# The two norms around mixer 2 made in halves of 256 tokens, with some weight low parts moved to GpSimd

## The reference, cut to what matters

```python
# end of block 1
x = x + 0.5 * swiglu(rms_norm(x, ffn2_norm), ffn2_w_gate, ffn2_w_up, ffn2_w_down)
# block 2
sh1, sc1, g1, sh2, sc2, g2 = jnp.split(mod, 6, axis=-1)
h = _rms(x, norm1_w) * (1 + sc1) + sh1                  # norm "p1"
u, q, k, v = jnp.split(h @ w_in, ...)                   # "q2" is computed first
... # S5 and sliding-window attention give "mixed"
x = x + g1 * (mixed @ w_out)                            # "w_out2"
h2 = _rms(x, norm2_w) * (1 + sc2) + sh2                 # norm "p2"
x = x + g2 * _conv_ffn(h2, w_up, conv_w, conv_b, w_down)  # "ffn3"
```

## Time and profile before

| | |
|---|---|
| median of 3 runs | 1794.73 us (1794.62 to 1794.98) |
| the profiled execution | 1793.39 us, its span 1791.9 us |
| PE busy | 1763.9 us, 98% |
| DVE busy | 1069.7 us, 60% |
| ACT busy | 729.3 us, 41% |
| POOL busy | 186.1 us, 10% |
| granted clock of PE | 0.999 over the span |

### The profile page before, as it was taken

How to read it: one execution, slowest core, us unless ns; L and a number is a source line. 1 busy time by engine, 2 the same in 40 slices (tenths; PEclk the granted TensorE clock), 3 DMA queues, 4 the chain that set the end, 5 groups by cost and what they waited for, 6 DMA issues and landing times. The chain is left out here.

```text
span 1791.9 us, 23429 instructions
## 1 busy us (share of the span) xinstructions
PE 1763.9 (98%) x8822; PEld 1437.1 (80%) x8822; DVE 1069.7 (60%) x1507; ACT 729.3 (41%) x1001; POOL 186.1 (10%) x239
## 2 busy tenths in 40 slices
PE   9999999999999999999999999999999999999998
PEld 6888888888887777788877888887986788888887
DVE  7666546655655676656888743436595655566433
ACT  4222222333435877423333222225465355555322
POOL 4222001210000000005211110210000300000000
PEclk9999999999999999999999999999999999999999
DMA  7777423343222121224554552325122222222232
GB/s 246 238 221 221 134 74 96 98 138 99 90 95 94 48 66 53 71 94 150 173 188 125 158 158 66 107 93 187 68 79 68 93 95 94 94 94 82 94 95 81
DMA packets 171694, 206.81 MB, mean 115 GB/s; under 512 B 18404, under 2 KB 150114, under 8 KB 171106
## 3 DMA queue, kind: packets, MB, share of 16 engines
q1 hardware_dynamic: 144994, 161.97, 27.9%
q0 software_dynamic: 12640, 38.55, 6.7%
q10 hardware_dynamic: 13984, 5.27, 1.1%
HBM read 190.29 MB, written 17.56 MB: 116 GB/s over the span
## 5 line engine op out<-in xcount | busy, mean ns | idle before, releaser
L692 ACT CAST w_hi<-w_raw 128x2048 fp32r<-128x2048 f32 x158 | 301.8, 1911 | 722.4 <-PE bank L2004 360.9
L1188 DVE TENSOR_TENSOR w_lo<-w_raw,w_hi 128x2048 fp32r<-128x2048 f32 x158 | 367.3, 2325 | 358.4 <-ACT w_hi L692 357.7
L2004 PE MATMUL bank<-h_hi,w_hi 128*128 128x512 f32 x1056 | 412.3, 390 | 3.5 <-DVE w_lo L1188 2.2
L2004 PE MATMUL bank<-h_hi,w_lo 128*128 128x512 f32 x1056 | 411.1, 389 | 0.0
L2004 PE MATMUL bank<-h_lo,w_hi 128*128 128x512 f32 x1056 | 325.4, 389 | 1.6 <-DVE h_lo L1231 1.6
L2004 PEld LDWEIGHTS bank<-h_hi,w_hi 128*128 128x128 f32 x1056 | 198.2, 188 | 49.5 <-issue 3.4
L2004 PEld LDWEIGHTS bank<-h_lo,w_hi 128*128 128x128 f32 x1056 | 198.2, 188 | 43.3 <-DVE h_lo L1231 2.0
L2004 PEld LDWEIGHTS bank<-h_hi,w_lo 128*128 128x128 f32 x1056 | 198.3, 188 | 41.0
L1961 PE MATMUL bank<-hid_hi,w_hi 128*128 128x512 f32 x528 | 205.6, 389 | 0.0
L1961 PE MATMUL bank<-hid_hi,w_lo 128*128 128x512 f32 x528 | 205.4, 389 | 0.0
L1961 PE MATMUL bank<-hid_lo,w_hi 128*128 128x512 f32 x528 | 205.4, 389 | 0.0
(11 more groups left out here) (442 smaller groups left out, 2464.8 us busy)
## 6 DMA issues: line engine op xcount, KB each, us to landing
w_raw<-in_w_in SPq DMA_DIRECT2D x29, 1024.0 KB, 5.0
mod_raw<-in_w_mod POOLq DMA_DIRECT2D x96, 256.0 KB, 4.1
w_raw<-in_ffn_w_gate SPq DMA_DIRECT2D x22, 1024.0 KB, 5.2
w_raw<-in_ffn_w_up SPq DMA_DIRECT2D x22, 1024.0 KB, 5.2
w_raw<-in_w_up SPq DMA_DIRECT2D x22, 1024.0 KB, 4.9
w_raw<-in_ffn_w_down SPq DMA_DIRECT2D x16, 768.0 KB, 4.6
w_raw<-in_ffn_w_down SPq DMA_DIRECT2D x16, 640.0 KB, 4.0
w_raw<-in_w_out SPq DMA_DIRECT2D x8, 1024.0 KB, 5.0
```

The lines of the kernel that those rows point to most:

```text
L692: act.copy(w_hi[i % 2][:], w_raw[i % 2][:]).then_inc(S("w_hi_done"), 1)
L1188: dve.tensor_tensor(w_lo[s][:], w_raw[s][:], w_hi[s][:].bitcast(F32), ALU.subtract).then_inc(S("w_split"), 1)
L2004: mm = pe.matmul(bank[:], w[:, k, at], h[:, k, :], start=k == first and part == 0 and i == 0, stop=k == last and part == 1)
```

## The change

Both norms are cut into two halves of 256 tokens.

- **First half early.** The last product group before each norm is made half by half. In `ffn2`, tiles 6 and 7 are closed one panel earlier, DVE adds that part to `x` (512 wide), and the last panel goes, half by half, to other banks and is added by `half_x2`. In `w_out2`, tile 7 is made in two halves. PE issues the three sums of half 0 between the two halves (`half_sums`).
- **Items.** The norm then makes 16 items (k, half) of 128 x 256, in the order of `ITEMS`. DVE issues the adds for half 1 among the first items, and refines half 1's root after item 3.
- **Products.** `q2` is made item by item in both its panels, 512 columns to a product as before. Step 0 of `ffn3` is made by `first_step`: all its products have 256 columns, and parts of the up panel stand between gate items 4 to 7.
- **Low parts on POOL.** The low parts of three weight panels (both of `q2`, and the up panel of `ffn3`'s step 0) are made by POOL (`low_part`) instead of DVE. POOL's load of `bias` comes after two of them.
- **The rest.** ACT loads the table of the reciprocal root ahead of norm p1 with a small activation; the 18 idle products are gone; the cast of the up panel of `ffn3`'s step 0 is made in two pieces with an item between.

```diff
...
+        HALF = [slice(c * T // 2, (c + 1) * T // 2) for c in range(2)]
+        IN_HALVES = {"ffn2": 2, "mix2": 1}
+        ITEMS = {"p1": [(k, c) for ks in (range(4), range(4, KD)) for c in range(2) for k in ks],
+                 "p2": [(k, c) for c in range(2) for k in range(KD)]}
+        HALF_SUMS = 3
+        HALF_SQ = {"p1": 4, "p2": 3}
...
+        def last_bank(k, c):
+            return B[((4, 6), (5, 4))[k % 2][c]]
+        def tile7_bank(c):
+            return B[(0, 4)[c]]
+        def half_sum(name, c):
+            return B[{"p1": (7, 5), "p2": (7, 6)}[name][c]][:, HALF[c]]
+        def slot(s):
+            return tmp[:, 2 + (s // 2 + 2) % 4, HALF[s % 2]]
...
+            def low_part(n):
+                pool.wait_ge(S("w_hi_done"), n + 1)
+                pool.wait_ge(S("w_split"), n)
+                pool.tensor_tensor(w_lo[n % 2][:], w_raw[n % 2][:], w_hi[n % 2][:].bitcast(F32), ALU.subtract).then_inc(S("w_split"), 1)
             norm("p1", "ffn2")
+            low_part(BASE["mix2"])
+            low_part(BASE["mix2"] + 1)
             wait_x(pool, "ffn2", KD - 1)
             pool.wait_ge(S("band_stored"), 16 * BESIDE_STEPS)
             pool.dma_start(bias[:], bass.AP(band_dram, P - 1, [[BAND - 1, P], [P * BAND, NQ], [1, 2 * P]])).then_inc(S("bias_landed"), 16)
             norm("p2", "mix2")
+            low_part(BASE["ffn3"] + 1)
...
+            def half_square(before, k, halves):
+                wait_x(act, before, k, halves[-1])
+                at = slice(HALF[halves[0]].start, HALF[halves[-1]].stop)
+                act.activation(tmp[:, 2 + k % 2, at], x[:, k, at], ACT.Square).then_inc(S("norm_sq"), 1)
+            def half_root(name, c):
+                act.wait_ge(S("norm_summed"), NORM_SUM[name] + HALF_SUMS * (c + 1))
+                act.activation(rstd[:, HALF[c]], half_sum(name, c), ACT.Abs_reciprocal_sqrt, scale=1.0 / D, bias=eps_col).then_inc(S("norm_root"), 1)
+            def half_cast(name, shift, items):
+                for s in items:
+                    k, c = ITEMS[name][s]
+                    act.wait_ge(S("norm_h"), NORM_H[name] + s + 1)
+                    act.activation(h_hi[:, k, HALF[c]], slot(s), ACT.Identity, bias=shift(k)).then_inc(S("norm_hi"), 1)
...
-            norm("p1", x, lambda eng, k: wait_x(eng, "ffn2", k), panel=BASE["mix2"] + 1, shift=lambda k: mod[:, k:k + 1])
+            done(act.activation(stat[:, 95:96], eps_col, ACT.Abs_reciprocal_sqrt))
+            shift1 = lambda k: mod[:, k:k + 1]
+            half_square("ffn2", 6, (0, ))
+            half_square("ffn2", 7, (0, ))
+            half_root("p1", 0)
+            half_cast("p1", shift1, (0, 1))
+            split(BASE["mix2"] + 1)
+            half_square("ffn2", 6, (1, ))
+            half_square("ffn2", 7, (1, ))
+            half_cast("p1", shift1, (2, 3))
+            half_root("p1", 1)
+            half_cast("p1", shift1, range(4, 2 * KD))
...
-            norm("p2", x, lambda eng, k: wait_x(eng, "mix2", k), panel=BASE["ffn3"] + 1, shift=lambda k: mod[:, 24 + k:25 + k])
+            shift2 = lambda k: mod[:, 24 + k:25 + k]
+            half_square("mix2", 6, (0, 1))
+            half_square("mix2", 7, (0, ))
+            half_root("p2", 0)
+            half_cast("p2", shift2, (0, 1))
+            half_square("mix2", 7, (1, ))
+            half_cast("p2", shift2, (2, ))
+            half_root("p2", 1)
+            half_cast("p2", shift2, (3, ))
+            n = BASE["ffn3"] + 1
+            act.wait_ge(S(f"w_landed{n % 2}"), 16 * (n // 2 + 1))
+            act.wait_ge(S("pe_done"), used(n - 2))
+            for part in range(2):
+                at = slice(part * PANEL // 2, (part + 1) * PANEL // 2)
+                ins = act.copy(w_hi[n % 2][:, at], w_raw[n % 2][:, at])
+                if part:
+                    ins.then_inc(S("w_hi_done"), 1)
+                half_cast("p2", shift2, (4 + part, ))
+            half_cast("p2", shift2, range(6, 2 * KD))
...
+            def half_root(name, c):
+                at = HALF[c]
+                v, vr, r = tmp[:, 0, at], tmp[:, 1, at], rstd[:, at]
+                dve.wait_ge(S("norm_root"), NORM_ROOT[name] + c + 1)
+                done(dve.scalar_tensor_tensor(v, half_sum(name, c), eps_width_col[D], r, ALU.add, ALU.mult))
+                done(dve.scalar_tensor_tensor(vr, v, -0.5 / D, r, ALU.mult, ALU.mult))
+                done(dve.scalar_tensor_tensor(r, vr, 1.5, r, ALU.add, ALU.mult))
+            def half_h(name, gain, s):
+                k, c = ITEMS[name][s]
+                if s >= 8:
+                    dve.wait_ge(S("norm_split"), NORM[name] + s - 7)
+                dve.scalar_tensor_tensor(slot(s), x[:, k, HALF[c]], gain(k), rstd[:, HALF[c]], ALU.mult, ALU.mult).then_inc(S("norm_h"), 1)
+            def half_lo(name, shift, s):
+                k, c = ITEMS[name][s]
+                dve.wait_ge(S("norm_hi"), NORM[name] + s + 1)
+                dve.scalar_tensor_tensor(h_lo[:, k, HALF[c]], slot(s), shift(k), h_hi[:, k, HALF[c]].bitcast(F32), ALU.add, ALU.subtract).then_inc(S("norm_split"), 1)
...
+            def half_x2(c, ks):
+                for k in ks:
+                    product = tmp[:, 5, HALF[k % 2]] if c else tmp[:, 4 + k % 2, HALF[c]]
+                    dve.wait_ge(S("pe_done"), used(BASE["mix2"] - 1, 2 * c + k % 2 + 1))
+                    done(dve.tensor_tensor(product, last_bank(k, c)[:, HALF[c]], rstd[:, HALF[c]], ALU.mult))
+                    dve.scalar_tensor_tensor(x[:, k, HALF[c]], product, 0.5, x[:, k, HALF[c]], ALU.mult, ALU.add).then_inc(S("ffn2_x"), 1)
             def down(name, factor, beside=()):
                 base = BASE[name] + 2 * GU_STEPS
                 for c in range(DOWN_PANELS):
-                    if c % 4 == 3:
+                    if name == "ffn2" and c == DOWN_PANELS - 2:
+                        for k in (6, 7):
+                            product = tmp[:, 4 + k % 2, :]
+                            dve.wait_ge(S("pe_done"), used(base + c))
+                            done(dve.tensor_tensor(product, down_bank(name, k)[:], rstd[:], ALU.mult))
+                            done(dve.scalar_tensor_tensor(x[:, k, :], product, factor(k), x[:, k, :], ALU.mult, ALU.add))
+                        continue
+                    if name == "ffn2" and c == DOWN_PANELS - 1:
+                        half_x2(0, (6, 7))
...
-            norm("p1", x, lambda k: gain2[:, 0, k:k + 1], lambda k: mod[:, k:k + 1], panel=BASE["mix2"] + 1)
+            p1 = lambda s: half_h("p1", lambda k: gain2[:, 0, k:k + 1], s)
+            p1_lo = lambda s: half_lo("p1", lambda k: mod[:, k:k + 1], s)
+            half_root("p1", 0)
+            p1(0)
+            p1(1)
+            p1_lo(0)
+            half_x2(1, (6, ))
+            p1_lo(1)
+            half_x2(1, (7, ))
+            wait_x(dve, "ffn2", KD - 1)
+            p1(2)
+            p1(3)
+            p1_lo(2)
+            p1_lo(3)
+            half_root("p1", 1)
+            for s in range(4, 2 * KD + 1):
+                if s < 2 * KD:
+                    p1(s)
+                if s > 4:
+                    p1_lo(s - 1)
...
+            def half_x7(c):
+                dve.wait_ge(S("pe_done"), used(n + 3, 3 + c))
+                dve.scalar_tensor_tensor(x[:, 7, HALF[c]], tile7_bank(c)[:, HALF[c]], mod[:, 23:24], x[:, 7, HALF[c]],
+                                         ALU.mult, ALU.add).then_inc(S("mix2_x"), 1)
+            p2 = lambda s: half_h("p2", lambda k: gain2[:, 1, k:k + 1], s)
+            p2_lo = lambda s: half_lo("p2", lambda k: mod[:, 24 + k:25 + k], s)
+            half_x7(0)
+            half_root("p2", 0)
+            p2(0)
+            p2(1)
+            p2_lo(0)
+            half_x7(1)
+            p2_lo(1)
+            p2(2)
+            p2(3)
+            p2_lo(2)
+            half_root("p2", 1)
+            for s in range(4, 2 * KD + 1):
+                if s < 2 * KD:
+                    p2(s)
+                p2_lo(s - 1)
...
+            def half_sums(name, c, squares):
+                bank = half_sum(name, c)
+                pe.wait_ge(S("norm_added"), ADDED.index(name) + 1)
+                pe.matmul(bank, ones[:], tmp[:, 0, HALF[c]], start=True, stop=False).then_inc(S("norm_summed"), 1)
+                for k, n in zip((6, 7), squares):
+                    pe.wait_ge(S("norm_sq"), NORM_SQ[name] + n)
+                    pe.matmul(bank, ones[:], tmp[:, 2 + k % 2, HALF[c]], start=False, stop=k == 7).then_inc(S("norm_summed"), 1)
...
+                            if first and c == 7:
+                                for half in range(2):
+                                    for t in range(2):
+                                        if (half, t) == (1, 1):
+                                            wait_x(pe, "ffn2", 6, 0)
+                                        terms = half_terms(base + c, kn, PC, t * P, half, hid_hi, hid_lo, k0)
```

(94 more changed lines are left out.)

62 lines of the change are left out of this document (35 added, 27 removed).

## The result

| | before | after |
|---|---|---|
| median of 7 runs each, us | 1794.69 (1791.55 to 1796.57) | 1799.88 (1798.38 to 1801.21) |
| profiled execution, us | 1793.39 | 1799.22 |
| its span, us; mean granted clock | 1791.9; 0.999 | 1797.7; 0.994 |

The changed kernel takes 1.0029 times as long, 95% interval 1.0020 to 1.0039: slower by 5.2 us. Forecast: 1799.8.

A forecast was written before the change was run, and what follows sets the result against it. PE bounds the kernel, losing time only at norms p1 and p2; POOL's long low parts would stop DVE there, outweighing the halves' gain. +3.8 and +1.2 make +5.0 on 1794.7: 1799.8 us, range 1796 to 1804.

The forecast's parts named there:

- The sum: Both norms: +3.8 us at p1 and +1.2 at p2 make +5.0 us; chance 0.42.
- Loss before, gain of the halves: Norms before lose 6.7 us (p1) and 6.8 (p2); halves would gain 11.3 if nothing else were lost.
- rival 1: Both norms: POOL blocks nothing for long; p1 -4.6 us, p2 -1.9, total -6.5, 1788.2 us; chance 0.22.
- First block: Norm p1, q2's first low part on POOL: holds DVE before its fourth step until 1217.1; PE idle 5.4 us.
- Second block: Norm p1, q2's second low part: POOL starts at 1226.5, holds DVE until 1231.1 before item 2; PE idle 3.9 us.
- p1 in all: Norm p1 would end at 1251.9 against 1248.07, +3.8 us.
- Third block, p2: Norm p2, up panel's low part: POOL holds DVE 1424.1 to 1428.7 before item 5's low part; PE idle 3.15 us.
- Idle products "save nothing by their going": Both norms: idle products cost nothing before, since PE's next product waited for ACT and DVE; removing them saves nothing.
- rival 2: Norm p1: blocks, and PE's clock falls in its long waits; +3.6 us and perhaps 0.5 more, 1804 us; chance 0.2.
- "Its clock never falls": Kernel before: PE is busy in every profile slice and its clock stays high throughout.
- "no row shows a fall": Kernel before: no profile row shows PE's clock falling, so none shows what idle time a fall takes.
- Rival 3: Both norms: blocks fall better than placed and cancel the halves' gain; within 2 us of before, 1795; chance 0.16.

The follow-up runs named there:

- Experiment 1: Changed kernel with all three POOL low parts given back to DVE, halves kept: 1788.49 us, 0.9972 of the kernel before.
- experiment 5: Changed kernel with 18 idle products put into PE's long waits (10 and 4 in p1, 4 in p2): 1800.02 us.
- experiment 7: Changed kernel with only q2's first low part given back to DVE, POOL keeping the other two: 1795.34 us.
- experiment 3: Kernel before with its 18 idle products removed and nothing else changed: 1795.76 us, 1.0010 of the kernel before.
- experiment 4: Changed kernel with POOL's low_part replaced by two fills with zeros, so POOL writes but reads nothing: 1788.88 us.
- experiment 6: Changed kernel with each POOL low part made in eight instructions of 256 columns instead of one of 2048: 1791.26 us.
- experiment 8: Experiment 1 with half 1's root in p2 moved behind two more items on ACT and DVE: 1786.40 us, 0.9965 of the kernel before.

## Why the prediction was right, point by point

- **The sum.** +5.0 forecast, +5.8 between the profiled executions, +5.2 between the medians. The mechanism is the forecast one: POOL's long instructions stop DVE, and that outweighs what the halves gain. Part of the exactness is luck, as the points below show.
- **Loss before, gain of the halves.** Without long blocks my steps gave p1 33.0 and p2 34.7 us from the same events (rival 1: 37.6 less 4.6, 36.6 less 1.9). Experiment 1 has 33.3 and 34.4. The counting of products by row spacing held to half a microsecond.
- **Duration of `low_part`.** 4.6 forecast, between 3.6 and 5.2; 4.53 to 4.55 measured. For an add with N = 2048 "GPSIMD Engine Reference", section 3.1 of the Trainium skill, has 4497 ns, and the trace agrees: the subtraction took 4.53 us.
- **First block.** Forecast: before the fourth DVE step, PE idle for 5.4 us. Right in kind, 0.8 us less in size: the step was held 4.93 us, PE stood 4.61 and then did its sums on the lower clock (2.07 us; experiment 1's take 1.43).
- **Second block.** Forecast: POOL at 1226.5, item 2's `tmp` held, PE idle 3.9. Wrong in detail. PE's half 1 ran 1 us longer on the fallen clock and all of p1 began 0.5 us later, POOL came at 1228.30, DVE had both `tmp`s out by then, and the block caught the low parts instead: idle 1.99. What the clock cost on one side it seems to have given back on the other. Experiments 5 and 7 show the case that I forecast.
- **p1 in all.** +3.8 forecast, +4.5 measured. Idle in the two large waits 4.61 + 1.99 = 6.6, and PE's busy time times the missing clock in the stretches shown 1.25 + 0.92 + 1.72 = 3.9: 10.5 us, where the forecast had 10.1 of idle time alone. Nearly the same sum from other parts; the clock after the second block (0.57 in 1234 to 1238) is the part that no wait covered. That these parts add up to the forecast's is luck.
- **Third block, p2.** Forecast: PE idle 3.15 at item 5's low part, +1.2. Measured: DVE held 4.46 us as forecast, PE idle 1.23, as its products ahead of it ran on a fallen clock (0.66 and 0.50). With the clock high up to there the wait is 2.73 (experiment 7). p2 +0.7.
- **Idle products "save nothing by their going".** Right for what they save. That their going costs was left to rival 2 alone; experiment 3 puts it at 1.7 us in the kernel before (interval 0.2 to 3.4), where PE's wait is 4.75 us in one piece.
- **"Its clock never falls", "no row shows a fall".** Wrong. The trace of the kernel before has the clock at 0.66 in 1350 to 1355, soon after the wait of 2.9 us of the earlier trace rows, which ended at 1348.64; digits of tenths for 45 us hide it. So waits much shorter than the forecast's 4.9 us already went with a fall, which spoke for rival 2's fact.
- **Rival 1** (POOL blocks nothing for long) is false: experiments 1, 4 and 6.
- **Rival 2** (the clock falls too) had its fact right and its price wrong. The clock fell in both places of p1, and in p2 as well, but +3.6 us weren't paid on top: experiment 5 brought the clock back and the median stayed (1800.02). I had added the slower products to the blocks' idle times, while they mostly ran in their place. "TensorE: Matmul & The Clock Gate", section "Why this matters for your kernels", of the Trainium skill asks for no long idle gaps between bursts; the trace agrees that the clock falls after such a gap (4.61 us), and the three executions of p2 (experiment 7) add that what a fall costs hangs on whether PE would have waited anyway.
- **Rival 3** (the blocks fall better) came true for the second block alone: PE's idle time there was 1.9 us shorter, and the slower products took most of that back. The third fell where I had placed it; its idle time was shorter only because PE came to it late.

**What is shown and what is argued.** Shown: the halves gain 5.5 us; POOL's low parts cost 11.4; POOL's long subtraction beside DVE's steps is the cause, as writing alone costs nothing and pieces cost a quarter. "SBUF — State Buffer", section "Who interferes with whom", of the Trainium skill says that a DVE instruction with two SBUF inputs contends with a GpSimd instruction that reads SBUF, not with one that only writes it: the runs agree, with 4.93 us beside the subtraction and 0.69 beside the fill. That a fall under a wait costs nothing and one behind it 1.5 us is read from three kernels with the same p2 code apart from the idle products, one execution each. Only argued: that in p1 the second block caught the low parts, and not item 2's `tmp`, because of the clock. It fits experiments 5 and 7, but no run changed the clock alone without moving POOL's start. And why experiment 5's shorter p1 (by 1.5 us) doesn't show in its median stays open; that is half of the spread of its runs (1797.52 to 1801.01).

Much of such a spread goes with the clock. The 22 executions of the kernel before of the second group have mean granted clocks of 0.995 to 1.000: the four at 1.000 took 1791.6 to 1792.9 us, the two at 0.995 took 1796.0 and 1797.2. So a local time has to be read together with the clock that its execution had there.

## What to carry to other kernels

Work that is moved to an engine with nothing to do isn't free if the two engines can't run side by side: look in the trace for a pair of their instructions that overlap in time, see which of their forms stretch, and price the moved instruction by its length on the chain of the engine that it stops. If it must go there, cut it into pieces as short as the other engine's steps: that turned 8.8 us into 2.3 in p1. And charge a fallen TensorE clock only where PE isn't about to wait anyway: ask what the slowed products' successor waits for. Before a gain is put down to a change, see whether it lies in the stretch that was changed: experiment 8's doesn't.

## What the runs showed of the hardware that was not expected

- POOL fills 128x2048 f32 in 1.81 us, beside DVE steps with two SBUF inputs that keep their 0.42 and 0.69 us.
- Eight POOL pieces of 128x256 took 6.6 to 6.9 us in all beside DVE, where one instruction over the same 2048 elements took 4.54; DVE steps beside them took 0.8 to 1.2 us instead of 0.4 to 0.7.
- With nearly the same short PE waits (1.16 us at most) the clock stayed at 1.00 in p2 of experiment 1, but fell (to 0.66 and 0.67 in 1420 to 1425) in p2 of experiments 4 and 6: those two p2 times are 1.5 us longer than experiment 1's 34.35. What decides it stays open.
